# A decoder step on one core: ScalarE squares each pair of head blocks two jobs ahead of its root instead of one, in the opening of each layer's tail

## The reference, cut to what matters

```python
ret = _rmsnorm(o_ret) * silu(ga)                      # layer 0, four heads of 128
dif = _rmsnorm(o_dif, g_diff) * (1.0 - lam_init)      # layer 0, four heads of 128
o = _rmsnorm(o, g_norm) * silu(r)                     # layer 1, four heads of 256
y = mix @ w_out
x = x + gate * _rmsnorm(y, g_post_mix)
h = _modulate(x, g_pre_ffn, shift, scale)
x = x + gate * _rmsnorm(_conv_ffn(h), g_post_ffn)
```

## Time and profile before

| | us |
|---|---|
| median of three runs | 3332.23 (3328.47 to 3340.8) |
| the profiled execution's own time | 3327.27 |
| its span | 3325.5 |
| PE busy | 2997.9 (90% of the span) |
| DVE busy | 1541.5 (46%) |
| ACT busy | 1069.1 (32%) |

### The profile page before, as it was taken

One profiled execution on the slowest core, in us unless ns is written; L12 is line 12 of the kernel. 1 busy time (PEld: TensorE's weight loads), 2 busy tenths in 40 slices (PEclk: granted clock), 3 DMA queues, 4 the chain that ended last, 5 costly groups with the idle time before them and its releaser, 6 DMA issues. The chain is left out here.

```text
span 3325.5 us, 51269 instructions
## 1 busy us (share of the span) xinstructions
PE 2997.9 (90%) x19508; PEld 2740.0 (82%) x19508; DVE 1541.5 (46%) x2318; ACT 1069.1 (32%) x1963; POOL 114.4 (3%) x133
## 2 busy tenths in 40 slices
PE   6999876886999999999998989587599999999996
PEld 4899852444889999999988989366399999999995
DVE  4243034565374455444465100675646454444556
ACT  4112112445353332333334111342345322333322
POOL 0000000000000000000000000352000000000000
PEclk9999987988999999999999999798899999999998
DMA  5332256872131111111123211233432111111113
GB/s 225 135 142 96 77 189 236 294 282 90 60 127 45 50 38 44 50 44 50 38 72 134 71 62 44 94 126 109 152 107 90 48 43 47 45 42 50 38 45 115
DMA packets 142142, 319.83 MB, mean 96 GB/s; under 512 B 12385, under 2 KB 75330, under 8 KB 133586
## 3 DMA queue, kind: packets, MB, share of 16 engines
q1 hardware_dynamic: 101330, 249.29, 21.4%
q10 hardware_dynamic: 40704, 69.09, 5.9%
HBM read 272.69 MB, written 45.64 MB: 96 GB/s over the span
## 5 line engine op out<-in xcount | busy, mean ns | idle before, releaser
L250 PE MATMUL f_acc<-h_hi,f_hi 128*128 128x352 f32 x1632 | 537.5, 329 | 12.3 <-issue 6.6
L250 PE MATMUL f_acc<-h_hi,f_lo 128*128 128x352 f32 x1632 | 531.6, 326 | 0.0
L250 PE MATMUL f_acc<-h_lo,f_hi 128*128 128x352 f32 x1632 | 528.5, 324 | 0.0
L250 PE MATMUL f_acc<-m_hi,f_hi 128*128 128x352 f32 x1248 | 410.1, 329 | 4.3 <-DVE m_lo L1556 3.3
L250 PE MATMUL f_acc<-m_hi,f_lo 128*128 128x352 f32 x1248 | 405.1, 325 | 0.0
L250 PE MATMUL f_acc<-m_lo,f_hi 128*128 128x352 f32 x1248 | 402.7, 323 | 0.0
L250 PE MATMUL f_acc<-f_ghi,f_hi 128*128 128x352 f32 x1056 | 342.2, 324 | 8.5 <-DVE y L1657 8.0
L250 PE MATMUL f_acc<-f_glo,f_hi 128*128 128x352 f32 x1056 | 339.5, 321 | 0.0
L250 PE MATMUL f_acc<-f_ghi,f_lo 128*128 128x352 f32 x1056 | 339.0, 321 | 0.0
L250 PEld LDWEIGHTS f_acc<-h_hi,f_hi 128*128 128x128 f32 x1632 | 310.5, 190 | 15.3 <-issue 9.2
L1650 DVE TENSOR_TENSOR y<-y,f_acc 128x1056 f32<-128x1056 f32 x160 | 200.3, 1252 | 263.9 <-PE f_acc L250 263.9
(11 more groups left out here) (362 smaller groups left out, 5045.7 us busy)
## 6 DMA issues: line engine op xcount, KB each, us to landing
f_st<-w_ffn SPq DMA_DIRECT2D x132, 512.0 KB, 3.4
kt<-cache_k SPq DMA_DIRECT2D x128, 256.0 KB, 5.3
att_vt<-cache_v SPq DMA_DIRECT2D x128, 256.0 KB, 5.6
gla_ada_w<-w_ada SPq DMA_DIRECT2D x16, 1024.0 KB, 5.4
x<-y ACTq DMA_DIRECT2D x9, 1408.0 KB, 5.5
ret_ada_w<-w_ada ACTq DMA_DIRECT2D x12, 1024.0 KB, 6.6
y<-w_qkv SPq DMA_DIRECT2D x10, 1024.0 KB, 5.9
open_ada_w<-w_ada SPq DMA_DIRECT2D x8, 1024.0 KB, 14.8
```

The costliest lines, as they stand in the source:

```text
L250: last = nc.tensor.matmul(out, a(kk), b(kk), start=(n == 0), stop=(n == 3 * nk - 1))
```

## The change

The order of ScalarE's instructions in the opening is written anew; no instruction is added or removed, and no other engine's order changes. In the prologue, square 4 moves ahead of high 1 and square 5 ahead of `round_unit(1)`. In the loop, the turn of job j squares job j+2 in place of job j+1.

```diff
--- before.py
+++ after.py
@@ -1265,17 +1265,18 @@
             head_square(3)
             head_hi(0)
             head_root(2)
+            head_square(4)
             head_hi(1)
             head_root(3)
+            head_square(5)
             round_unit(1)
             head_hi(2)
-            head_square(4)
             head_hi(3)
             round_unit(2)
             for j in range(4, JOBS):
                 head_root(j)
-                if j + 1 < JOBS:
-                    head_square(j + 1)
+                if j + 2 < JOBS:
+                    head_square(j + 2)
                 if j > 4:
                     head_hi(j - 1)
                 if j in (5, 6, 8, 10):
```

## The result

The changed kernel takes 3297.6 us (median of six executions, 3293.4 to 3304.9) against 3332.6 us for the kernel before (six executions, 3328.5 to 3340.8). The ratio is 0.9894, with a 95% interval of 0.9876 to 0.9911: 35 us faster by the medians, 30 to 41 by the interval. The forecast was 3296, the range 3287 to 3312.

What follows compares the result with a forecast made beforehand. PE was taken to bound the steady part, and chains handed between engines the two openings. Gains of 20.65 us in layer 0 and 15.75 in layer 1, together 36.4, off the 3332.23 median gave a forecast of 3296, range 3287 to 3312.

Steps and rivals of the forecast that it cites:

- The bound: Whole kernel: PE bounds the steady part; the two openings are chains between engines with no engine full.
- Sums 4 and 5, piece 0: Start of each opening: earlier squares leave low parts last, so piece 0 starts 4.3 us earlier in layer 0, 2.65 in layer 1.
- Piece 0 to piece 1: Each opening: the 2.44 us wait between sums 6 and 7 goes; gain 2.5 us in layer 0, 2.3 in layer 1.
- piece 0, whose start I leave as it was: Clock assumption in each opening: full clock for all but piece 0, which still takes 4.60 us to sums 6.
- rival C: Openings: clock stays low through all pieces; slower by 13 us, at 3345; chance 0.02.
- Pieces 1 to 2 and 2 to 3: Rounds: one wait moves to sums 9 and 11, the second goes; gains 5.1 and 6.65 us (layer 0), 4.3 and 5.6 (layer 1).
- Pieces 3 to 5: End of each opening: full clock, 12.6 to 12.75 us including the wait behind; gain 2.1 us in layer 0, 0.9 in layer 1.
- The clock: Openings: one gap of 1.8 or 1.2 us per round keeps full clock except at piece 0; granted clock above 0.9.
- A: Rounds: the clock still falls in each; gain only 22.75 us, median 3309.5; chance 0.22, mixtures with the forecast included.
- B: Openings: VectorE takes ScalarE's place, low 7 or unit 3's rest holding PE; costs 8 us, 3304; chance 0.08.
- D: Rounds: something unseen holds them, only piece 0 and one round gain, 12 to 21.2 us; 3311 to 3320; chance 0.06.
- The total: Both openings: gains of 20.65 us in layer 0 and 15.75 in layer 1, together 36.4, giving 3296.

Runs made afterwards that it cites:

- e6: Changed kernel with unit 1's rounding on ScalarE moved behind high 3 and its rest on VectorE behind low 3; 3296.9 us, ratio 0.9899.
- e3: Changed kernel with throwaway matmuls on PE ahead of piece 0 only: 5 before sums 4, 5 before sums 5, 12 after; 3301.8 us, ratio 0.9907.
- e7: Changed kernel with both edits: takes of pieces 1 and 2 later, and unit 1's rounding and rest later; 3287.9 us, ratio 0.9869.
- e4: Changed kernel with ScalarE's takes of pieces 1 and 2 moved from turns 6 and 8 to turns 7 and 9; 3293.6 us, ratio 0.9883.
- e5: Kernel before with throwaway matmuls on PE in its waits for squares ahead of sums 7 to 11; 3326.0 us, ratio 0.9974.
- e1: Prologue part alone: squares 4 and 5 moved as in the change, loop still squaring one job ahead as in the kernel before; 3330.8 us, ratio 1.0.
- e8: Changed kernel run again with nothing edited, in the second session; 3300.8 us, ratio 0.9904.
- e2: Loop part alone on the kernel before: turn 4 squares jobs 5 and 6, then the loop squares two ahead; 3310.6 us, ratio 0.9931.

## Why the prediction was right, point by point

**The bound.** Right. The openings were chains with no full engine, and all that was gained in the openings, but for one low spell, arrived at the end of the span. The steady part did not move: 600 us of it hold 3725 matmuls in the kernel before and 3726 in both executions of the changed kernel.

**Sums 4 and 5, piece 0.** Right to 0.1 us in both layers (4.2 and 2.6), and for the reason given: low 3 on VectorE is now last, and e6 moved piece 0 by moving what stood ahead of low 3. One detail was off without cost: sums 4 and 5 took 1.45 us each, not 2.71, so sums 5 too waited for their square (1.47 us in layer 0, 0.88 in layer 1). Four waits for squares were left behind sums 3 in each layer and not three.

**Piece 0 to piece 1.** The order was right, since sums 6 and 7 run together, but the size was off: 1.2 in each layer for 2.5 and 2.3. The step that failed is "piece 0, whose start I leave as it was". With three sums and three waits ahead of it, the last of 2.45 and 3.71 us, piece 0 took 6.1 and 5.9 us to sums 6 instead of 4.6. e3 showed that the idle time is the cause by filling all three gaps of layer 0: 3.97 us. It is the thin stretch as a whole and not the last wait alone, as e7's piece 0 took 5.5 us behind no wait. What rival C described for the whole opening happened for this one piece.

**Pieces 1 to 2 and 2 to 3.** Right to 0.1 us in all four terms, and e4 confirmed the mechanism by taking the moved wait away. The gaps themselves were 1.96 and 1.38 us for the 1.8 and 1.2 of the prediction.

**Pieces 3 to 5.** Mis-sized: 0.1 for 2.1 in layer 0, 0.5 for 0.9 in layer 1. In layer 0 the clock fell once more behind the last gap of 1.96 us (sums 11 took 1.64 and pieces 3 to 5 13.7 us). In layer 1, behind gaps of 1.38, they took 12.1, at the full clock as forecast; there 0.5 is all, since 12.1 + 1.0 is 13.1 and not 12.75: 72 steps of 0.161 leave out that the first matmul's step is 0.43 us (the second starts that much later) and that the last one's end, 0.32 us behind its start, is what the take waits for.

**The clock.** The forecast was that the full level would hold for all but piece 0. It held for pieces 1 and 2 and the pieces behind them in layer 1, not for piece 3 in layer 0. The openings came to a granted clock of 0.90 and 0.93, where above 0.9 was forecast. The same waits did not give the same spells: piece 0 took 6.1 us in e5 and 4.6 before, and sums 5 2.71 us in e1, e4 and e7 and 1.45 in e6 and the changed kernel, while e8 repeated the changed kernel's pattern. The Trainium skill, "TensorE: Matmul & The Clock Gate", in its part on the clock gate, has it that the number of slow matmuls at a start varies from run to run of one kernel. These traces agree between kernels with the same work at that place; within one kernel the only pair, the changed kernel and e8, did not vary.

**The rivals.** A was right in places and wrong as a whole: 22.75 was its sum and 31.5 came. B did not happen: PE waited for no low part at piece 3, even in e7. D did not happen: both rounds gained in both layers. Counted from the end of sums 3, as the forecast did, the openings came out at 48.2 and 45.3 us for its 45 and 44: longer by the four mis-sized terms.

**The total.** The sum of 36.4 was too large by 5 against the openings' 31.5, and the forecast of 3296 was met to 1.6 us because the medians lie 35 apart. That closeness is partly luck: in the second session the same kernel was 31.1 us ahead, at 3300.8 us.

## What to carry to other kernels

Where two engines hand work to and fro (sums, root, square), put the producer's next step so that it stands ahead of the first instruction that waits for the other engine's long work; look for what stands behind such a wait in an in-order queue, and count a wait that only moves to the next consumer as kept, less what it now hides. Look also behind the wait that is removed for what will be last (here a rounding and a rest that stood ahead of low 3): e4 and e6, read off the waits that were left, gave another 12 us. Cost a piece behind idle gaps at both levels of TensorE's clock: no safe size of gap was found here, as a wait of 1.47 us was followed by the low level in three executions of six.

## What the runs showed of the hardware that was not expected

- Filling PE's waits with throwaway matmuls gave 7.9 us in the openings of the kernel before and 0.9 in those of the changed kernel, where only the waits ahead of piece 0 were filled and the low spell came back at a later gap.
- A gap of 1.96 us ahead of sums 9 or 11 in layer 0 left the clock up in some places and not in others. Sums 9 took 1.45 us in the changed kernel's two executions and in e6, but 2.20 in e2 and 2.48 in e3. Sums 11 were slowed in all five, least in the changed kernel (1.64 and 1.54) and most in e6 (2.60). A gap of 1.38 us never brought it down in layer 1 (sums 9 and 11 at 1.45 in five profiled executions). What decides it stays open.
- The size of one gap is not what decides it: 1.47 us ahead of sums 5 in layer 0, with short sums and waits before it, was followed by sums at 2.71 in e1, e4 and e7 and at 1.45 in three others.
- A wait of 3.3 us behind layer 1's opening cost nothing in the profiled execution of the kernel before and 1.4 to 3.1 us in the nine others that were profiled (988 to 978 matmuls in the same time, for 997).
